# Expert stage of a decoder step: small and large items for singles and pairs, wider weight rows, every sixth weight subtraction on POOL

## The chip, the cores and the metric

The kernel runs on one core of a Trainium2 chip. The metric is the device time of one execution in microseconds (us). The engines are named as in the profile: PE (TensorE, matmuls), PEld (its weight loads), DVE (VectorE), ACT (ScalarE), POOL (GpSimd), SP (SyncE, which issues the weight loads). SBUF is the memory on the core with 128 partitions, PSUM holds the results of matmuls in eight banks of 512 columns.

## The reference

One inference step of a two-layer decoder on 256 prompt tokens and 8 sample tokens, in fp32. Layer 0 is attention and a dense SwiGLU, layer 1 a convolution module and a mixture of experts, and each sub-layer is modulated and normalised. The change is in the mixture of experts alone:

```python
logits = (h @ w_router + b_router).astype(jnp.float32)
top_l, top_e = lax.top_k(logits, MOE_TOPK)          # 2 of 8 experts for each token
gates = jax.nn.softmax(top_l, axis=-1)
...
def expert_group(args):
    xg, e = args
    return (jax.nn.silu(xg @ w1[e]) * (xg @ w3[e])) @ w2[e]
```

w1 and w3 of an expert are 1024 x 3584, w2 is 3584 x 1024, 44.04 MB together. The 264 tokens make 528 assignments. The reference's own router, evaluated on its inputs, gives the experts 0 to 7 these numbers of tokens: 5, 67, 165, 3, 200, 18, 15, 55.

## The kernel before

**Precision.** fp32 weights and activations are split into a high half (rounded to fp32r) and a low half (what remains), and a product is made of three fp32r matmuls: high by high, high by low, low by high. So each weight tile passes three engines: SP loads it into one of seven slots of `ring` (128 x 2048, 1 MB), ACT casts it to `w_hi` (L1061), DVE subtracts `w_hi` from it to `w_lo` (L1683), PE multiplies by both. The slot is free for SP when `w_lo` is written; a buffer of `w_hi` and `w_lo` is free for ACT when PE has used it.

**Units.** An expert has `ES` = 42 slots, and a slot is two units of 1024 columns, so 84 units. `SPLITS` = 4 buffers hold units. The slots of w1 and w3 hold four rows of 512 columns (2 KB pieces of a weight row), those of w2 two rows of 1024 columns (4 KB). `EXPERT_SLOTS` is the order: w1 and w3 of hidden chunk j (512 of 3584 columns, seven chunks), then w2 of chunk j - 1.

**Items.** DVE computes the list of items at run time. Of each expert up to 128 tokens are a single item; an expert of 1 to 7 with more than 128 tokens is a pair item, two groups of 128 that share each load. Expert 0 begins before the list is known. All engines run the same program of passes, `passes`: `item` for each single, `between`, then `pair` for each pair.

**A single pass** on PE: for each unit 6 matmuls with 128 tokens stationary and 512 weight columns moving (L777 for w1 and w3, L768 for w2). Behind a chunk's w3, ACT takes silu of h1 (L1071), DVE multiplies by h3 (L1718), PE transposes the product (L792, `TURN` units later), ACT and DVE split it (L1075, L1722). At the end of a pass come the gather of the next item's tokens (L741: 24 fp32 matmuls, tokens by a one-hot selection matrix), its split (L1039, L1664), and the y matmuls (L803: eight, results by the gates back to token order), each added to `zT` by DVE (L1676) before the second next may run.

**A pair pass**: w1 and w3 tiles are stationary and 2 x 128 tokens move (L852, 24 matmuls of 256 columns in a unit), w2 moves (L839, 12 matmuls of 512 columns in a unit). Subtractions are L1755, casts L1090, the gather is L813 (48 fp32r matmuls of 256 columns) and y is L873 and L874.

**Order.** Every engine runs its own instructions strictly in the order in which they are written. POOL makes constants and stores and has nothing to do in the expert stage. SP issues load n when slot n - 7 is free.

Of the kernel before, what the change touches and what calls it, by code (L numbers as in the profile page):

```python
# [16 lines left out]
F32 = mybir.dt.float32  # L17
# [22 lines left out]
EJ = FE // 512  # L40
GROUPS = 3
ITEMS = GROUPS * NE
CANDS = ITEMS + NE
PAIRS = min(2 * T // (P + 1), NE - 1)
MIN_SINGLES = NE - PAIRS
MAX_ITEMS = NE + 1 + 2 * T // (2 * P + 1)
LIST = MAX_ITEMS + PAIRS + 1
# [20 lines left out]
EXPERT_SLOTS = []  # L68
for _j in range(EJ + 1):
    _kinds = (["w1", "w3"] if _j < EJ else []) + (["w2"] if _j else [])  # L70
    EXPERT_SLOTS += [(_k, _j - (_k == "w2"), _h) for _k in _kinds for _h in range(2)]
ES = len(EXPERT_SLOTS)
EU = ES * UNITS


def last_unit(kind, j):

    return UNITS * (EXPERT_SLOTS.index((kind, j, 1)) + 1) - 1


def build(nc, x_prompt, x_sample, cache_k, cache_v, state_conv, page_table, c_prompt, c_sample,
# [5 lines left out]
    with ctx:  # L87
# [17 lines left out]
        w_hi = sb("w_hi", [P, SPLITS, UW], F32R)  # L105
        w_lo = sb("w_lo", [P, SPLITS, UW], F32R)
# [10 lines left out]
        column_v = sb("column_v", [P, CANDS])  # L117
        expert_v = sb("expert_v", [P, CANDS])
# [16 lines left out]
        arena_w = 14900  # L135
# [81 lines left out]
        x_hi2 = sb("x_hi2", [P, KC, 2, P], F32R, at=moe)  # L217
        x_lo2 = sb("x_lo2", [P, KC, 2, P], F32R, at=moe)
        g_hi2 = sb("g_hi2", [P, 2, 4, 2 * P], F32R, at=moe)
        g_lo2 = sb("g_lo2", [P, 2, 4, 2 * P], F32R, at=moe)  # L220
        x_hi, x_lo = x_hi2[:, :, 0, :], x_lo2[:, :, 0, :]
        g_hi = g_hi2[:, :, :, :].rearrange("p i c n -> p i (c n)")[:, :, 0:512]
        g_lo = g_lo2[:, :, :, :].rearrange("p i c n -> p i (c n)")[:, :, 0:512]
        g2 = sb("g2", [P, 2 * 512], at=moe)
        g_tok = g2[:, 0:512]
        h_tok = sb("h_tok", [P, 3, D], at=moe)
# [1769 lines left out]
```

## Time and profile before

| | us |
|---|---|
| median of 3 runs | 2150.91 (2150.74 to 2153.38) |
| the profiled execution, span | 2147.9 |
| PE busy | 2005.3 |
| DVE busy | 1435.4 |
| ACT busy | 1039.7 |
| POOL busy | 17.0 |
| first and last matmul of the expert units | 771.2 and 2113.9 |

The span is from the first to the last instruction. Matmuls are pipelined, so that their busy times overlap and the time between the starts of two is what one costs. In the windows view a line has the stretch, its length, busy time and count of each engine, the granted clock of TensorE (1.00 is 2.4 GHz, 0.50 is 1.2 GHz), the share of time in which the DMA engines were busy, and GB/s. In groups of instructions a line has line, engine, operation, output and inputs by name and shape, count, busy us and mean ns, and the idle time before them with what ended it.

### The profile page before, as it was taken

How to read it: one execution, taken by the hardware profiler on the slowest of the kernel's cores; microseconds unless marked ns; L12 is line 12 of the kernel's file. 1: busy time of each engine (PE TensorE's matmuls, PEld its weight loads, DVE VectorE, ACT ScalarE, POOL GpSimd, SP SyncE). 2: the span in 40 equal slices, each digit the busy share in tenths (PEclk: the TensorE clock that was granted, in tenths of full speed). 3: DMA queues.
4: the chain of work that ended last, by engine and by line, in shares of the span. 5: the costliest groups of instructions: out<-in, count | busy, mean ns of one | idle time of the engine just before them, and what ended most of it. 6: DMA issues, size and time to landing. Idle time of an engine off the chain costs nothing.

```text
span 2147.9 us, 31958 instructions
## 1 busy us (share of the span) xinstructions
PE 2005.3 (93%) x12022; PEld 1697.5 (79%) x12022; DVE 1435.4 (67%) x1928; ACT 1039.7 (48%) x1253; POOL 17.0 (1%) x68
## 2 busy tenths in 40 slices
PE   4988689999798799999999999999989999999997
PEld 2964279999787677788787887878869999799995
DVE  2578455555797579799797897978845555455454
ACT  1212223443354258677676775767724444244442
POOL 1000000000000000000000000000000000000000
PEclk8986799999898779999999999999979999999999
DMA  9647686556635059899798897998935555355520
GB/s 304 210 152 261 242 260 203 177 177 203 189 104 181 33 201 359 302 331 357 278 355 322 316 359 280 354 332 304 358 121 195 185 189 195 109 187 181 193 79 21
DMA packets 270395, 491.71 MB, mean 229 GB/s; under 512 B 9134, under 2 KB 121206, under 8 KB 270269
## 3 DMA queue, kind: packets, MB, share of 16 engines
q1 hardware_dynamic: 269261, 485.89, 65.5%
q0 software_dynamic: 1024, 4.25, 0.6%
q8 instruction: 81, 1.33, 0.3%
q14 instruction: 29, 0.24, 0.0%
HBM read 486.71 MB, written 4.35 MB: 229 GB/s over the span
## 4 chain that ended last, share of the span: by engine, by line
PE 81%; DVE 4%; ACT 1%; DMA 1%; issue 1%; DVEq 0%; SPq 0%; POOL 0%; ACTq 0%
PE banks L777 22%; PE banks L852 15%; PE banks L768 11%; PE banks L442 10%; PE banks L839 7%; PE banks L741 3%; PE banks L652 3%; PE banks L673 2%; PE banks L813 2%; PE banks L514 1%; PE banks L792 1%; PE banks L803 1%; PE banks L491 1%; PE banks L471 1%; DMA arena<-in_state_conv_dram 1%
## 5 line engine op out<-in xcount | busy, mean ns | idle before, releaser
L1683 DVE TENSOR_TENSOR w_lo<-ring,w_hi 128x1024 fp32r<-128x1024 f32 x504 | 601.1, 1222 | 72.2 <-ACT w_hi L1061 71.8
L1061 ACT CAST w_hi<-ring 128x1024 fp32r<-128x1024 f32 x504 | 521.3, 1052 | 147.5 <-PE banks L777 116.8
L1755 DVE TENSOR_TENSOR w_lo<-ring,w_hi 128x1024 fp32r<-128x1024 f32 x168 | 205.0, 1224 | 209.9 <-ACT w_hi L1090 209.0
L1090 ACT CAST w_hi<-ring 128x1024 fp32r<-128x1024 f32 x168 | 175.3, 1048 | 232.5 <-PE banks L852 169.5
L777 PE MATMUL banks<-w_hi,x_hi 128*128 128x512 f32 x672 | 268.6, 400 | 4.4 <-DVE w_lo L1683 3.2
L777 PE MATMUL banks<-w_lo,x_hi 128*128 128x512 f32 x672 | 266.5, 397 | 0.0
L777 PE MATMUL banks<-w_hi,x_lo 128*128 128x512 f32 x672 | 266.4, 396 | 0.0
L442 PE MATMUL banks<-h_hi,w_hi 128*128 128x264 f32 x800 | 237.8, 297 | 29.1 <-DVEq L404 29.1
L852 PE MATMUL banks<-x_hi,w_hi 128*128 128x256 f32 x896 | 252.3, 282 | 6.6 <-DVE w_lo L1755 6.6
L852 PE MATMUL banks<-x_hi,w_lo 128*128 128x256 f32 x896 | 251.7, 281 | 0.0
L852 PE MATMUL banks<-x_lo,w_hi 128*128 128x256 f32 x896 | 251.5, 281 | 0.0
L442 PE MATMUL banks<-h_lo,w_hi 128*128 128x264 f32 x800 | 233.5, 292 | 0.0
L442 PE MATMUL banks<-h_hi,w_lo 128*128 128x264 f32 x800 | 233.2, 291 | 0.0
L916 ACT CAST w_hi<-ring 128x1024 fp32r<-128x1024 f32 x124 | 121.5, 1031 | 199.4 <-PE banks L442 93.3
L1168 DVE TENSOR_TENSOR w_lo<-ring,w_hi 128x1024 fp32r<-128x1024 f32 x124 | 143.8, 1204 | 106.6 <-ACT w_hi L916 106.0
L442 PEld LDWEIGHTS banks<-h_hi,w_hi 128*128 128x128 f32 x800 | 158.2, 198 | 31.1 <-DVEq L404 30.7
L852 PEld LDWEIGHTS banks<-x_hi,w_hi 128*128 128x128 f32 x896 | 170.0, 190 | 7.8 <-DVE w_lo L1755 7.3
L852 PEld LDWEIGHTS banks<-x_lo,w_hi 128*128 128x128 f32 x896 | 170.0, 190 | 0.5
L852 PEld LDWEIGHTS banks<-x_hi,w_lo 128*128 128x128 f32 x896 | 169.9, 190 | 0.0
L442 PEld LDWEIGHTS banks<-h_lo,w_hi 128*128 128x128 f32 x800 | 158.3, 198 | 0.4
L442 PEld LDWEIGHTS banks<-h_hi,w_lo 128*128 128x128 f32 x800 | 157.0, 196 | 0.0
L777 PEld LDWEIGHTS banks<-w_hi,x_hi 128*128 128x128 f32 x672 | 126.8, 189 | 37.2 <-issue 6.4
(339 smaller groups left out, 3093.9 us busy)
## 6 DMA issues: line engine op xcount, KB each, us to landing
ring<-in_moe_w_dram SPq DMA_DIRECT2D x336, 1024.0 KB, 6.2
ring<-in_ada_w_dram SPq DMA_DIRECT2D x48, 1024.0 KB, 5.8
ring<-in_ffn_w_dram SPq DMA_DIRECT2D x30, 1024.0 KB, 5.5
ring<-in_attn_w_qkv_dram SPq DMA_DIRECT2D x12, 1024.0 KB, 11.9
ring<-in_conv_w_pw_dram SPq DMA_DIRECT2D x12, 1024.0 KB, 9.7
ring<-in_cache_k_dram SPq DMA_DIRECT2D x16, 512.0 KB, 6.1
ring<-in_cache_v_dram SPq DMA_DIRECT2D x16, 512.0 KB, 7.1
ring<-in_attn_w_o_dram SPq DMA_DIRECT2D x4, 1024.0 KB, 9.1
```

The source lines that it names most:

```text
L442: mm = pe.matmul(bk[:, 0:T], w, x[:, k, :], start=(k == 0 and i == 0), stop=(k == KC - 1 and i == 2))
L652: mm = pe.matmul(two[m][:, 0:T], w, x[:, g, :], start=(g == 0 and i == 0), stop=(g == FM - 1 and i == 2))
L768: mm = pe.matmul(out_b[:, b], x[:, j % 2, a], y[:, b], start=(j == 0 and u == 0 and k == 0), stop=(j == EJ - 1 and u == 3 and k == 2))
L777: mm = pe.matmul(bk[:, :], x[:, 2 * u + kk, :], y[:, b], start=(u == 0 and kk == 0 and k == 0), stop=(u == 3 and kk == 1 and k == 2))
L839: mm = pe.matmul(out_p_b[g][:, b], x[:, j % 2, u, a], y[:, b], start=(j == 0 and u == 0 and k == 0), stop=(j == EJ - 1 and u == 3 and k == 2))
L852: mm = pe.matmul(bk, x[:, a], y[:, 2 * u + kk, :, :].rearrange("p g n -> p (g n)"), start=(u == 0 and kk == 0 and k == 0 and m % 2 == 0), ...
L916: act.copy(w_hi[:, (q * UNITS + u) % SPLITS, 0:e - o], ring[:, n % RING, o:e]).then_inc(ev("w_hi_ready"), 1)
L1061: act.copy(w_hi[:, n % SPLITS, :], ring[:, pos_of(s), o:o + UW]).then_inc(ev("moe_hi_ready"), 1)
L1090: act.copy(w_hi[:, n % SPLITS, :], ring[:, pos_of(s), o:o + UW]).then_inc(ev("moe_hi_ready"), 1)
L1168: dve.tensor_tensor(w_lo[:, i, 0:e - o], ring[:, n % RING, o:e], w_hi[:, i, 0:e - o].bitcast(F32), ALU.subtract).then_inc(ev("w_lo_ready"), 1)
L1683: dve.tensor_tensor(w_lo[:, n % SPLITS, :], ring[:, pos_of(s), o:o + UW], w_hi[:, n % SPLITS, :].bitcast(F32), ALU.subtract).then_inc(ev(" ...
L1755: dve.tensor_tensor(w_lo[:, n % SPLITS, :], ring[:, pos_of(s), o:o + UW], w_hi[:, n % SPLITS, :].bitcast(F32), ALU.subtract).then_inc(ev(" ...
```

## The change

- A **small item** has up to 64 tokens. Their high and low halves stand side by side as one stationary operand of 128 columns (`x_s`), so that a product takes two matmuls in place of three: (high, low) by `w_hi` and (high, low) by `w_lo`. The halves are added when the result is turned, by a matmul with a constant `joint` of 128 x 64.
- A **large item** has up to 128 tokens and three matmuls. There are no pairs: an expert's c tokens make c // 128 large items and for the rest a small one if it is at most 64, else a large one. All small ones run first.
- A unit is now a whole slot of 2048 columns. There are `WBUF` = 3 buffers for these. Chunks are 1024 hidden columns wide (the last 512), so that w1 and w3 slots hold two rows of 1024 (4 KB pieces). 
- **POOL subtracts** for slots 3, 9, 15, 21, 27, 33 and 39 (`POOL_UNITS`), DVE for the other 35. `wait_low` waits for the one or the other.
- The gather runs on fp32r halves of the tokens behind slot 38, four before the pass's end; y matmuls of an item run in two parts inside the next item's pass, behind slots 2 and 5, and DVE adds two banks at a time.
- The first three slots are cast and subtracted before the list is computed; tokens are split at once as they leave PSUM.

The diff's core:

```diff
+CHUNKS = ((0, 2), (2, 2), (4, 2), (6, 1))
+NCH = len(CHUNKS)
+WBUF = 3
...
+TURN_AT = [n + 2 for n in LAST_W3]
+Y_AT = (2, 5)
+POOL_UNITS = tuple(range(3, ES, 6))
+
+
+def lowered(n):
+
+    mine = [i for i in range(ES) if (i in POOL_UNITS) == (n % ES in POOL_UNITS)]
+    return n % ES in POOL_UNITS, len(mine), len(mine) * (n // ES) + mine.index(n % ES) + 1
+GATE_AT, GATE_ROWS_AT, NEXT_AT, GATHER_AT = 10, 24, 24, ES - 4
...
+        def wait_low(eng, w, n):
+            on_pool, each, count = lowered(n)
+            eng.wait_ge(ev("moe_pool_lo_ready" if on_pool else "moe_lo_ready"), each * w + count)
...
+            def gather(width, x_sel, done):
+
+                x = x_b[:, 0:2 * KC * width].rearrange("p (k s n) -> p k s n", k=KC, s=2)
                 for k in range(KC):
-                    for i, (t0, tn) in enumerate(TILES):
-                        mm = pe.matmul(xT_b[:, k * P:(k + 1) * P], h_tok[0:tn, i, k * P:(k + 1) * P], sel_t[0:tn, i, :],
-                                       start=(i == 0), stop=(i == 2))
+                    for s, h in enumerate((h_tok_hi, h_tok_lo)):
+                        for i, (t0, tn) in enumerate(TILES):
+                            mm = pe.matmul(x[:, k, s, :], h[i][0:tn, k * P:(k + 1) * P], x_sel[0:tn, i, :],
+                                           start=(i == 0), stop=(i == 2), skip_group_check=True)
...
+            def x_small(k, hi, lo):
+                x = x_s[:, k, :, :].rearrange("p s n -> p (s n)")
+                return (x, hi), (x, lo)
...
+            def x_large(k, hi, lo):
+                return (x_m[:, 0, k, :], hi), (x_m[:, 0, k, :], lo), (x_m[:, 1, k, :], hi)
...
+            def small(w, first=False):
+                for n in range(ES):
+                    if n == 0:
+                        pe.wait_ge(ev("small_x_ready"), 2 * w + 2)
+                    if n in (8, 20, 32):
+                        pe.wait_ge(ev("moe_h1_kept"), NCH * w + 1 + (8, 20, 32).index(n))
+                    if n in (12, 24, 34):
+                        pe.wait_ge(ev("moe_h3_kept"), NCH * w + 1 + (12, 24, 34).index(n))
+                    unit(w, n, x_small, g_small)
+                    if n in Y_AT and not first:
+                        y_part(w - 1, Y_AT.index(n))
...
+                    if n == GATHER_AT:
+                        pe.wait_ge(ev("moe_h3_kept"), NCH * w + NCH)
+                        gather_small(w + 1)
...
+            def cast(w, n):
+                act.wait_ge(slot_sem[pos_of(n)], w * (16 * ES // RING) + moe_loaded(n))
+                act.wait_ge(ev("moe_units_used"), ES * w + n + 1)
+                act.copy(w_unit(n)[0], ring[:, pos_of(n), :]).then_inc(ev("moe_hi_ready"), 1)
...
+                    if n not in POOL_UNITS:
+                        lower(w, n)
...
             def expert(e, w, s):
 
-                sp.wait_ge(ev("moe_lo_ready"), EU * w + UNITS * (s - RING + 1))
+                wait_low(sp, w, s - RING)
                 expert_load(e, s)
...
+            def lower(w, n):
+                pool.wait_ge(ev("moe_hi_ready"), ES * w + n + 1)
+                hi, lo = w_unit(n)
+                pool.tensor_tensor(lo, ring[:, pos_of(n), :], hi.bitcast(F32), ALU.subtract).then_inc(ev("moe_pool_lo_ready"), 1)
```

How the instructions move, at three places. DVE in the first units of a single pass, before (`x_lo` is the tokens' low half, the `zT` rows are the y additions of the item before):

```order
592 L1683 TENSOR_TENSOR w_lo<-ring,w_hi 128x1024
593 L1682 REGISTER_ALU
594 L1683 TENSOR_TENSOR w_lo<-ring,w_hi 128x1024
595 L1663 ISA
596 L1664 TENSOR_TENSOR x_lo<-banks,x_hi 128x4x128 x2
597 L1673 ISA
598 L1676 TENSOR_TENSOR zT<-zT,banks 128x264
599 L1673 REGISTER_ALU
600 L1676 TENSOR_TENSOR zT<-zT,banks 128x264
```

And after, the first subtractions of a small item's pass:

```order
579 L1591 TENSOR_TENSOR w_lo<-ring,w_hi 128x2048
580 L1589 REGISTER_ALU
581 L1591 TENSOR_TENSOR w_lo<-ring,w_hi 128x2048
582 L1589 REGISTER_ALU
583 L1591 TENSOR_TENSOR w_lo<-ring,w_hi 128x2048
584 L1739 ISA
585 L1742 TENSOR_TENSOR zT<-zT,banks 128x528 x2
```

Before, the y additions (eight of 264 columns) follow the fourth unit's subtraction; after, four of 528 stand in two places further in. The three subtractions shown last are slots 2, 4 and 5: slot 3 is missing, it is POOL's.

POOL in a small item's pass, after, where it had nothing before:

```order
52 L2005 ISA
53 L2007 TENSOR_TENSOR w_lo<-ring,w_hi 128x2048
54 L2005 REGISTER_ALU
55 L2007 TENSOR_TENSOR w_lo<-ring,w_hi 128x2048
56 L2005 REGISTER_ALU
57 L2007 TENSOR_TENSOR w_lo<-ring,w_hi 128x2048
```

These are the first three of the seven subtractions of a pass, one for each sixth slot.

PE at the end of a single pass, before (`hT` is the selection matrix or the kept output, L741 the gather, L803 the y matmuls):

```order
4284 L768 MATMUL banks<-w_hi,g_lo 128x512
4285 L741 MATMUL banks<-hT,h_tok 128x128 x24
4286 L803 MATMUL banks<-hT 128x264 x2
4287 L801 REGISTER_ALU
4288 L803 MATMUL banks<-hT 128x264
```

And after, at slot 38 of a small pass (the first of eight equal groups of the gather, L768) and at the pass's end:

```order
3931 L834 MATMUL banks<-w_lo,g_buf 128x512
...
3933 L768 MATMUL banks<-sel_s,h_hi 128x64 x2
3934 L768 MATMUL banks<-sel_s,h_tok_hi 128x64
3935 L768 MATMUL banks<-sel_s,h_lo 128x64 x2
3936 L768 MATMUL banks<-sel_s,h_tok_lo 128x64
...
3991 L834 MATMUL banks<-w_lo,g_buf 128x512
3992 L374 UNCONDITIONAL_BRANCH
```

The gather has moved ahead of the last three slots, and nothing but the branch stands between the last expert matmul of a pass and the next pass.

## Rows read from the trace of the kernel before

**Rows 1.** The page: its span, and the chain that ended last.

```profile
span 2147.9 us, 31958 instructions
...
PE 81%; DVE 4%; ACT 1%; DMA 1%; issue 1%; DVEq 0%; SPq 0%; POOL 0%; ACTq 0%
PE banks L777 22%; PE banks L852 15%; PE banks L768 11%; PE banks L442 10%; PE banks L839 7%; PE banks L741 3%; PE banks L652 3%; PE banks L673 2%; PE banks L813 2%; PE banks L514 1%; PE banks L792 1%; PE banks L803 1%; PE banks L491 1%; PE banks L471 1%; DMA arena<-in_state_conv_dram 1%
```

**Rows 2.** Windows: a stretch of a single pass, and one of a pair pass.

```profile
1062.00:1160.00 98.00, 98.00 (x435) 79.08 (x434) 88.92 (x86) 75.86 (x81) 0.00 (x0) 1.00 0.99 357
1610.00:1835.00 225.00, 225.00 (x1632) 211.57 (x1631) 118.27 (x111) 96.40 (x93) 0.00 (x0) 1.00 0.57 189
```

**Rows 3.** Timeline of PE (start, length) at pass ends, and L777's first start.

```profile
1030.87 8.40 PE L741 MATMUL banks<-hT,h_tok 128*128 128x128 f32 x48
1039.20 1.16 PE L803 MATMUL banks<-hT 128*128 128x264 f32 x4
1041.01 3.62 PE L803 MATMUL banks<-hT 128*128 128x264 f32 x12 [0.65 <-DVE zT L1676]
...
1166.11 8.40 PE L741 MATMUL banks<-hT,h_tok 128*128 128x128 f32 x48
...
L777 PE MATMUL banks<-w_hi,x_hi x672: 392/396/766, 771.2 to 1559.1; 128*128 128x512 f32 x168
```

**Rows 4.** Timeline of PE: two matmuls six apart, one unit.

```profile
1102.79 0.40 PE L768 MATMUL banks<-w_hi,g_hi 128*128 128x512 f32 x1
...
1104.19 0.40 PE L768 MATMUL banks<-w_hi,g_hi 128*128 128x512 f32 x1
```

**Rows 5.** Groups on DVE and ACT in the pass from 1030 to 1166 us.

```profile
L1683 DVE TENSOR_TENSOR w_lo<-ring,w_hi 128x1024 fp32r<-128x1024 f32 x86 | 102.8, 1223 | 12.9 <-ACT w_hi L1061 12.9
L1722 DVE TENSOR_TENSOR g_lo<-banks,g_hi 128x512 fp32r<-128x512 f32 x7 | 4.8, 691 | 0.5
...
L1061 ACT CAST w_hi<-ring 128x1024 fp32r<-128x1024 f32 x85 | 88.0, 1052 | 26.1 <-PE banks L777 20.4 <-PE banks L768 5.7
...
L1075 ACT CAST g_hi<-banks 128x512 fp32r<-128x512 f32 x7 | 4.1, 588 | 5.5 <-PE banks L792 5.5
```

**Rows 6.** Waits of SP's queue from 1060 to 1160 us: total, times, longest.

```profile
SPq L1864 <- DVE w_lo L1683: 77.4, 34, 3.3
```

**Rows 7.** DMA from 225 to 245 us in 40 slices, GB/s: cache loads.

```profile
GB/s 0 0 0 0 0 0 0 164 287 270 385 401 393 393 360 401 393 410 303 352 410 418 401 401 442 434 418 401 401 451 434 410 401 369 148 66 0 0 0 0
```

**Rows 8.** Groups on POOL.

```profile
L1961 POOL MEMSET zT<- 128x2112 f32 x1 | 1.9, 1858 | 69.8 <-DVEq L404 69.8
...
L1921 POOL TENSOR_SCALAR_AFFINE_SELECT arena<-arena 128x256 f32<-128x256 f32 x1 | 0.4, 400 | 0.1
...
L1921 POOL TENSOR_SCALAR_AFFINE_SELECT arena<-arena 128x128 f32<-128x128 f32 x1 | 0.3, 294 | 0.1
```

**Rows 9.** L1595 on DVE: duration ns, start.

```profile
L1595 DVE TENSOR_SCALAR xT<-xT x1: 1246/1246/1246, 746.5 to 746.5; 128x2112 f32<-128x2112 f32 x1
```

**Rows 10.** Timeline: first weight load and last matmul of a pair's gather.

```profile
1834.84 0.19 PEld L813 LDWEIGHTS banks<-sel_p,h_hi 128*128 128x128 f32 x1
...
1843.56 0.28 PE L813 MATMUL banks<-sel_p,h_tok_lo 8*128 8x256 f32 x1
```

**Rows 11.** Timeline of PE: last gather of the singles, first pair matmul.

```profile
1571.43 8.40 PE L741 MATMUL banks<-hT,h_tok 128*128 128x128 f32 x48
...
1608.16 0.58 PE L852 MATMUL banks<-x_hi,w_hi 128*128 128x256 f32 x1 [3.98 <-DVE w_lo L1755]
```

**Rows 12.** The chain behind the last expert matmul (start, length).

```profile
2113.88 1.24 DVE out_p L1775
...
2122.11 0.46 PE banks L874 x2
```

**Rows 13.** Windows: a stretch without matmuls, and the next but one.

```profile
540.00:543.00 3.00, 0.00 (x0) 0.00 (x0) 2.96 (x6) 0.34 (x1) 0.00 (x0) 1.00 1.10 349
...
546.00:549.00 3.00, 2.93 (x13) 2.94 (x14) 2.46 (x4) 0.00 (x0) 0.00 (x0) 0.50 1.10 347
```

More of the change, by code:

```diff
@@ L877, in _, with gather_small, gather_large, y_part @@
-            passes(pe, expert, pair, lambda last: gather_pair(0))
+                        mm.then_inc(done, 1)
+            def gather_small(w):
+                pe.wait_ge(ev("small_sel_ready"), w + 1)
+                gather(SMALL, sel_s, ev("small_x_filled"))
+            def gather_large(d):
+                pe.wait_ge(ev("large_sel_ready"), d + 1)
+                gather(P, sel_m, ev("large_x_filled"))
+            def y_part(w, part):
+                if part == 0:
+                    pe.wait_ge(ev("moe_out_kept"), w + 1)
+                    pe.wait_ge(ev("moe_gs_kept"), w + 1)
+                    pe.wait_ge(ev("moe_y_zeroed"), 1)
+                else:
+                    pe.wait_ge(ev("moe_y_added"), 4 * w + 2)
+                for k in range(4 * part, 4 * part + 4):
+                    mm = pe.matmul(y_bank(k), out_sb[:, k * P:(k + 1) * P], gs[:, :], start=True, stop=True)
+                mm.then_inc(ev("moe_y_filled"), 1)
@@ L878, in _, with between @@
+            gather_small(0)
+            def between(n_small):
+                pe.wait_ge(ev("small_x_ready"), 2 * n_small + 4)
+                gather_large(0)
+            last = items(pe, lambda: small(0, first=True), lambda d: small(d + 1), between,
+                         lambda d, n_small: large(d, n_small + d + 1))
+            y_part(last, 0)
+            y_part(last, 1)
             norm(4, zT, hT, range(KC))
@@ L1110, in _, with between @@
+            for n in range(WBUF):
+                cast(0, n)
+            keep_small(0)
+            def between(n_small):
+                keep_large(0)
+            last = items(act, lambda: small(0, first=True), lambda d: small(d + 1), between,
+                         lambda d, n_small: large(d, n_small + d + 1))
+            keep_out(last)
             norm(4, zT[:, :, :], hT[:, :, :])
@@ new lines, in _ @@
+            dve.wait_ge(small_step, 1)
+            for i in range(3):
+                last = dve.tensor_scalar(sel_s[:, i, :], iota_slot[:, 0:SMALL], rank_c[:, i:i + 1], None, ALU.is_equal)
+            last.then_inc(ev("small_sel_ready"), 1)
+            for n in range(WBUF):
+                lower(0, n)
+            step(dve.memset(scan[:, :, :], 0.0))
+            step(dve.tensor_scalar(xT[:, :, :], xT[:, :, :], ALPHA, None, ALU.mult))
+            step(dve.tensor_scalar(cnt[:, 0:1], cnt[:, 0:1], float(-SMALL), None, ALU.add))
@@ L1789, in _, with between @@
+            def between(n_small):
+                dve.wait_ge(ev("moe_gsel_ready"), n_small + 1)
+                select_large(0, n_small + 1)
+            last = items(dve, lambda: small(0, first=True), lambda d: small(d + 1), between,
+                         lambda d, n_small: large(d, n_small + d + 1))
+            add_y(last, 0)
+            add_y(last, 1)
             dve.drain()
```

802 lines of the change are left out of this document (377 added, 425 removed).

## The prediction

> **What bounds the kernel now.** I read the page first: PE is busy for 93% of a span of 2147.9 us and makes 81% of the chain that ended last, with the expert stage's matmul lines L777 and L852 at its head [rows 1]. Everything the change touches is that stage, so I next read it in stretches. In a single pass (one item alone) PE is busy throughout at full granted clock while DMA moves 357 GB/s; in a pair pass PE is again full and DMA moves 189 GB/s [rows 2]. The starts of two gathers, one pass apart, give the period of a single pass: 1166.11 - 1030.87 = 135.2 us [rows 3]. Six matmuls of 512 columns take 1.40 us, 0.233 us each [rows 4], so the 84 units of a pass take 117.6 us; the other 17.6 us are a gather (8.4), the y matmuls (1039.2 to 1044.6, 5.4) and transposes (3.8) [rows 3]. PE sets both kinds of pass. DMA is not late: in a stretch of 100 us SP waits 77 for DVE to free a slot [rows 6].
>
> The stage begins with PE's first unit at 771.2 and ends with the last matmul at 2113.88: 1342.7 us for six single passes and two pair passes [rows 3, 12]. The counts follow from 504 and 168 subtractions at 84 a pass.
>
> **The new list of passes.** The router's counts, 5, 67, 165, 3, 200, 18, 15 and 55, give small items for experts 0, 3, 5, 6, 7 and the rest of expert 2: six. Large ones are experts 1, 2 and twice 4: four. Ten passes instead of eight, so 440 MB of expert weights instead of 352, and 420 instead of 336 slots to split.
>
> **A large pass.** The arithmetic per slot is two old units: 12 matmuls, 2.80 us [rows 4]. 42 slots: 117.6 us. Transposes stay 3.8. The y matmuls of the pass before need no wait between them any more, and eight at 0.29 (four took 1.16 before the first wait [rows 3]) are 2.3 us. The gather becomes 48 fp32r matmuls of 128 columns; 48 of 256 columns took 8.9 us [rows 10], half the columns would be 4.5 at least, and I take 6.4. Sum 130.1 us. DVE and ACT have the time: one subtraction of 2048 columns, from 690 ns at 512 and 1223 at 1024, is 2.29 us, and one cast, from 588 and 1052, 1.98 us [rows 5].
>
> What is new is **the slot that POOL subtracts**. With three buffers instead of four half-sized ones, the cast of slot n starts when PE has used slot n-3. PE then has 5.6 us of other work. Cast 1.98, POOL's subtraction, and about 0.4 for three hand-overs must fit into it, so POOL may take 3.2 us. No row shows POOL subtracting. Its one-tensor rows run at 0.84 ns a column (affine select 400 - 294 over 128 columns; a memset of 2112 in 1.86 us) plus 0.19 [rows 8]: 1.9 us if both reads and the write overlapped, 3.6 if the two reads follow one another, 5.4 if all three do. I take the middle of the last two, 4.5 us. Then PE stalls 4.5 - 3.2 = 1.3 us seven times a pass, 9.1 us. At the first turn (behind slot 9, which is POOL's) the product on DVE comes behind subtraction 10 and is about 0.8 us late, other turns 0.2 twice. A large pass: 130.1 + 9.1 + 1.2 = 140.4, four 562 us.
>
> The Trainium skill prices this one operation: "GPSIMD Engine Reference", section on elementwise cycle accounting, measured a two-input fp32 operation of 2048 columns at 4497 ns on GpSimd and 2293 on DVE. By it the sum is the one above; no row here shows it.
>
> **A small pass.** Its eight matmuls a slot are 1.87 us of PE, 78.4 us a pass; with 56 small turn matmuls, gather and y about 95. ACT: 42 casts of 1.98 are 83, with copies about 97. DMA: a burst of 1 MB loads ran at 390 to 410 GB/s [rows 7], so 44.04 MB need 110 us. If DVE and POOL subtract independently, DVE has 35 x 2.29 = 80 and 10.6 of its own, and DMA is last. If they can't overlap, the two together have 35 x 2.29 + 7 x 4.5 = 111.7, 14 hand-overs of 0.13 (1.8), the part of DVE's own work that no POOL slot covers (7.4 of 10.6: the y additions behind slot 8, two products and the gate copy lie beside POOL), and about 4 where ACT's copies delay a cast by more than the 0.5 us slack of three buffers. Sum 125 us, last.
>
> Which one? No row shows both reading SBUF in earnest at once. But DVE's one-input L1595 does 2112 columns in 1.25 us, 0.59 ns a column [rows 9], where a two-input subtraction needs 1.04 [rows 5]. This looks like an engine with two read paths, both taken by the subtraction of two SBUF tensors, and POOL must get its operands somewhere. I take no overlap, and keep 110 as the other end. Six small passes: 6 x 125 = 750. The first has three subtractions done ahead, and DVE computes the list among the others, which I set equal.
>
> The Trainium skill speaks against this edit more plainly. "SBUF — State Buffer", section "Who interferes with whom", says that a DVE instruction with two SBUF inputs and a GpSimd instruction that reads SBUF share a read interface, and the one issued second waits until the first is done. By that rule six passes are the 750 above, without it some 660. No row of this trace can show it.
>
> **Start, bridge, end.** The new first gather has 48 short fp32r matmuls instead of 24 fp32 ones, and three slots are cast and subtracted before it is done: I take -4, within 5 either way, so the first unit is at 767. Between the last single and the first pair PE has 36.8 us from the last gather to the first pair unit [rows 11]. Between small and large there is one gather (6.4), two copies of x (1.1 behind the last half), one cast (1.98) and one subtraction (2.29), and as PE idles for some 5 us the clock may fall: 15 us. Behind the last expert matmul (2113.88) 34.0 us are left; the 16 y matmuls from 2115.1 to 2122.6 [rows 12] become 8, their 7.4 us become 2.3: 29.
>
> **The sum.** 767 + 750 + 15 + 562 + 29 = 2123 us of span, against 2147.9. The median of the runs is 3.0 above the profiled span: 2126 us, -1.2%. The gain is small because the two pair passes (1608.2 to 2113.9, 506 us) turn into four large ones (562), and because a small pass wins only 10 us on 135, where its matmuls alone would win 39.
>
> **Rivals.** *Overlap*: POOL and DVE don't hinder one another; DMA bounds small passes at 110 and one or two for the boundary. Six, with seven slots loaded ahead (-18), 648 to 655 instead of 750. Time 2126 - 100 = 2026. For it: no row shows an obstacle. Against: the widths argument above. Chance 0.22.
>
> *Faster POOL without overlap*: at 3.6 us a slot, 0.9 x 42 = 38 in small passes and 0.9 x 28 = 25 in large: 2063. Chance 0.08.
>
> *Slower, POOL's price*: the same mechanism pays 7 us for each 0.1 us that POOL takes longer (70 slots, all on a path that ends last). The gain of 25 is used up at 4.85 us; at the bound of 5.4 the time is 2126 + 63 = 2189. For it: three streams that don't overlap at all is what the rates of one-stream rows can't exclude. Chance 0.15.
>
> *Slower, the clock*: small passes leave PE idle a third of the time. In the trace the clock stayed at its higher level in a stretch without any matmul and was at the lower, 1.2 GHz, soon after [rows 13]. At 1.2 GHz a slot needs 3.73 us and the pass some 187 instead of 125; more than two fifths of one pass at that level in total eats the gain. Against it: PE's longest gap in my small pass is 4.5 - 1.87 = 2.6 us, behind which a dense burst follows, and at 1.2 GHz PE would be busy all the time. Chance 0.05; at a fifth of the small time, 2126 + 75 = 2201.
>
> **Chances and range.** My forecast's own case has 0.50, within 2106 to 2148, and I give it 0.42 faster, 0.06 same, 0.02 slower. (About 0.2%, 4.3 us, is what a measurement of this kernel can tell from no change.) With the rivals: faster 0.42 + 0.22 + 0.08 = 0.72, same 0.07, slower 0.21. The range 2020 to 2175 takes in the overlap case and the lower half of the expensive POOL; the clock and POOL's upper bound lie outside.
>
> **What would show each step.** POOL's row should read about 4.5 us for 128x2048, and DVE's subtractions 2.29. If there is no overlap, DVE's instruction next to a POOL one either reads longer than 2.29 or waits, and a small pass's DMA moves about 350 GB/s, not 400. A large pass should take 140 us with seven idle gaps of PE released by POOL's w_lo, and a small pass 125, released by DVE or POOL, not DMA. I am wrong in the number of passes if there are not 420 loads; wrong in the rest if large passes don't show the stall, or if the page shows PE's clock below 0.9 in small passes.

## The result, and the profile after

The changed kernel takes 2235.02 us (median of 4 runs, 2226.63 to 2239.54) against 2150.82 (median of 4) for the kernel before, a ratio of 1.0385 with a 95% interval of 1.0356 to 1.0414. I had forecast 2126 us and a range up to 2175. It is slower by 84 us, where I had it faster by 25.

The page of the profiled execution: span, busy time, the chain that ended last, and the costliest groups (columns as in [rows 5]).

```profile
span 2237.8 us, 27910 instructions
...
PE 1977.1 (88%) x10382; PEld 1605.1 (72%) x10382; DVE 1538.6 (69%) x1534; ACT 1153.0 (52%) x1020; POOL 340.2 (15%) x141
...
issue 47%; PE 24%; POOL 12%; DVE 3%; ACT 2%; DMA 0%; POOLq 0%; DVEq 0%; SPq 0%; ACTq 0%
...
L1591 DVE TENSOR_TENSOR w_lo<-ring,w_hi 128x2048 fp32r<-128x2048 f32 x350 | 911.1, 2631 | 333.2 <-ACT w_hi L1074 333.2
L1074 ACT CAST w_hi<-ring 128x2048 fp32r<-128x2048 f32 x420 | 796.5, 1909 | 406.1 <-PE banks L846 295.4
L2007 POOL TENSOR_TENSOR w_lo<-ring,w_hi 128x2048 fp32r<-128x2048 f32 x70 | 322.4, 4606 | 1118.5 <-ACT w_hi L1074 1118.5
L846 PE MATMUL banks<-w_hi,x_s 128*128 128x512 f32 x672 | 298.9, 445 | 104.9 <-POOL w_lo L2007 85.0
```

In [rows 1] PE made 81% of the chain. This chain follows POOL's own queue: POOL has 12% of it, and most of the 47% called issue is the time between two of POOL's subtractions, to which the profile puts no cause, so the shares don't say what bounds the stage. The last group does say something: the small items' matmuls wait 85 us for POOL's low halves. The count is as forecast: 350 + 70 = 420 subtractions, ten passes.

ACT copies a pass's finished output (L1101) once in the next pass, so the starts of these copies give the periods. Timeline rows (start, length) of a small and a large pass:

```profile
911.30 1.01 ACT L1101 COPY hT<-banks 128x1024 f32<-128x1024 f32 x1
1045.89 1.00 ACT L1101 COPY hT<-banks 128x1024 f32<-128x1024 f32 x1
...
1768.44 1.01 ACT L1101 COPY hT<-banks 128x1024 f32<-128x1024 f32 x1
1914.94 1.01 ACT L1101 COPY hT<-banks 128x1024 f32<-128x1024 f32 x1
```

134.6 us for this small pass (the four between the first and the fifth copy are 134.6, 139.4, 136.0, 140.6, mean 137.7), 146.5 for this large one. These two periods are the measure in the experiments: small is the mean of those four, large the mean of the second and third of the four large passes.

**One POOL slot in a small pass** (timeline of POOL, DVE, PE and ACT; in brackets the idle time before and who ended it):

```profile
986.23 4.62 POOL L2007 TENSOR_TENSOR w_lo<-ring,w_hi 128x2048 fp32r<-128x2048 f32 x1 [12.21 <-ACT w_hi L1074]
...
986.34 0.43 DVE L1747 COPY hT<-banks 128x264 f32<-128x264 f32 x1
988.39 6.81 DVE L1591 TENSOR_TENSOR w_lo<-ring,w_hi 128x2048 fp32r<-128x2048 f32 x2 [1.62 <-ACT w_hi L1074]
...
990.90 0.50 PE L846 MATMUL banks<-w_hi,x_s 128*128 128x512 f32 x1 [2.31 <-POOL w_lo L2007]
...
993.74 1.90 ACT L1074 CAST w_hi<-ring 128x2048 fp32r<-128x2048 f32 x1 [3.21 <-PE banks L846]
```

POOL works from 986.2 to 990.85. DVE's copy out of PSUM (L1747) runs beside it in its usual 0.43 us. The next two subtractions take 6.81 us together instead of 4.57, and the first of them is the long one: it ends 2.15 us after POOL, nearly its usual length, so it stood still until POOL was done. PE is idle for 2.31 us and ACT, which waits for a free buffer, for 3.21.

**The gather in a small pass** (timeline of PE, then windows, in which the third number from the end is the granted clock, then DVE):

```profile
1025.25 0.30 PE L768 MATMUL banks<-sel_s,h_hi 128*128 128x64 f32 x2
...
1036.95 0.80 PE L834 MATMUL banks<-w_hi,g_buf 128*128 128x512 f32 x1
```

```profile
1025.20:1028.20 3.00, 3.00 (x18) 2.54 (x17) 3.00 (x1) 0.00 (x0) 1.06 (x1) 1.00 1.02 410
1029.70:1037.20 7.50, 7.50 (x26) 6.47 (x26) 2.29 (x1) 1.90 (x3) 0.00 (x0) 0.50 0.97 338
```

```profile
1031.01 2.29 DVE L1591 TENSOR_TENSOR w_lo<-ring,w_hi 128x2048 fp32r<-128x2048 f32 x1 [1.37 <-ACT w_hi L1074]
1042.38 2.29 DVE L1591 TENSOR_TENSOR w_lo<-ring,w_hi 128x2048 fp32r<-128x2048 f32 x1 [9.08 <-ACT w_hi L1074]
```

The 48 short matmuls take 11.70 us here, 10.9 to 12.6 in the other small passes. PE is busy all the time, yet the granted clock falls from 1.00 to 0.50 (2.4 to 1.2 GHz) in the middle of them. While they run PE frees no buffer. ACT casts one more slot at 1029.08, and the next only at 1040.44, when the first slot behind the gather, at half clock, has freed its buffer; DVE is idle for 9.08 us. ACT's own order stops it too: the cast of the gathered tokens stands ahead of the next weight cast and waits until 1037.06 for the gather.

### The profile page after: what moved, and what is told of

It reads as the page before. It is cut to its first block, busy times and chain, and to the rows that moved or that the text cites. A ratio compares the mean times of both kernels' runs of the same rounds, so it can differ in the third digit from the quotient of the medians.

```text
span 2237.8 us, 27910 instructions
## 1 busy us (share of the span) xinstructions
PE 1977.1 (88%) x10382; PEld 1605.1 (72%) x10382; DVE 1538.6 (69%) x1534; ACT 1153.0 (52%) x1020; POOL 340.2 (15%) x141
## 3 DMA queue, kind: packets, MB, share of 16 engines
q0 software_dynamic: 1024, 4.25, 0.6%
## 4 chain that ended last, share of the span: by engine, by line
issue 47%; PE 24%; POOL 12%; DVE 3%; ACT 2%; DMA 0%; POOLq 0%; DVEq 0%; SPq 0%; ACTq 0%
POOL w_lo L2007 12%; PE banks L471 11%; PE banks L681 3%; PE banks L702 2%; PE banks L846 2%; PE banks L834 1%; PE banks L768 1%; PE banks L543 1%; ACT w_hi L1074 1%; PE banks L520 1%; PE banks L500 1%; DVE w_lo L1214 1%; PE banks L804 0%; DMA ring<-in_attn_w_o_dram 0%; DVE rstd L1298 0%
## 5 line engine op out<-in xcount | busy, mean ns | idle before, releaser
L1591 DVE TENSOR_TENSOR w_lo<-ring,w_hi 128x2048 fp32r<-128x2048 f32 x350 | 911.1, 2631 | 333.2 <-ACT w_hi L1074 333.2
L1074 ACT CAST w_hi<-ring 128x2048 fp32r<-128x2048 f32 x420 | 796.5, 1909 | 406.1 <-PE banks L846 295.4
L2007 POOL TENSOR_TENSOR w_lo<-ring,w_hi 128x2048 fp32r<-128x2048 f32 x70 | 322.4, 4606 | 1118.5 <-ACT w_hi L1074 1118.5
L846 PE MATMUL banks<-w_hi,x_s 128*128 128x512 f32 x672 | 298.9, 445 | 104.9 <-POOL w_lo L2007 85.0
L846 PE MATMUL banks<-w_hi,x_m 128*128 128x512 f32 x896 | 290.5, 397 | 28.2 <-POOL w_lo L2007 22.4
L834 PE MATMUL banks<-w_hi,g_buf 128*128 128x512 f32 x784 | 297.1, 420 | 3.1 <-DVE w_lo L1591 2.5
L846 PE MATMUL banks<-w_lo,x_s 128*128 128x512 f32 x672 | 284.8, 424 | 0.0
L834 PE MATMUL banks<-w_lo,g_buf 128*128 128x512 f32 x560 | 231.2, 413 | 0.0
L964 ACT CAST w_hi<-ring 128x1024 fp32r<-128x1024 f32 x124 | 121.4, 1031 | 198.6 <-PE banks L471 92.6
L1214 DVE TENSOR_TENSOR w_lo<-ring,w_hi 128x1024 fp32r<-128x1024 f32 x124 | 143.9, 1205 | 105.7 <-ACT w_hi L964 104.8
```

Source lines behind the costliest of these rows:

```text
L834: mm = pe.matmul(out_b[:, b, :], g, y, start=(p == 0 and t == 0 and i == 0), stop=(p == NCH - 1 and t == 2 * last + 1 and i == len(g_passe ...
L846: mm = pe.matmul(bk[:, b, :], x, y, start=(k == 0 and i == 0), stop=(k == KC - 1 and i == len(x_passes(k, hi, lo)) - 1), skip_group_check= ...
L964: act.copy(w_hi[:, (q * UNITS + u) % SPLITS, 0:e - o], ring[:, n % RING, o:e]).then_inc(ev("w_hi_ready"), 1)
L1074: act.copy(w_unit(n)[0], ring[:, pos_of(n), :]).then_inc(ev("moe_hi_ready"), 1)
L1214: dve.tensor_tensor(w_lo[:, i, 0:e - o], ring[:, n % RING, o:e], w_hi[:, i, 0:e - o].bitcast(F32), ALU.subtract).then_inc(ev("w_lo_ready"), 1)
L1591: dve.tensor_tensor(lo, ring[:, pos_of(n), :], hi.bitcast(F32), ALU.subtract).then_inc(ev("moe_lo_ready"), 1)
```

## The experiments

Two questions were open: what does POOL's slot cost and by which mechanism, and what does the gather cost. All ratios are against the kernel before.

| | small | large | time | ratio (95%) |
|---|---|---|---|---|
| the changed kernel | 137.7 | 146.5 | 2235.0 | 1.0385 (1.0356 to 1.0414) |
| no subtraction on POOL | 122.7 | 138.4 | 2109.7 | 0.9808 (0.9769 to 0.9848) |
| gather in four groups | 133.7 | 141.0 | 2186.7 | 1.0174 (1.0146 to 1.0203) |
| both of these | 120.0 | 133.6 | 2083.8 | 0.9696 (0.9668 to 0.9724) |
| DVE copies, POOL subtracts | 136.4 | 143.4 | 2217.4 | 1.0320 (1.0284 to 1.0355) |
| a third of the gather | 129.1 | 132.9 | 2106.3 | 0.9788 (0.9772 to 0.9805) |
| POOL subtracts half a slot | 121.1 | 138.3 | 2102.0 | 0.9781 (0.9765 to 0.9797) |
| POOL works for nobody | 140.0 | 150.7 | 2249.4 | 1.0463 (1.0445 to 1.0481) |
| both edits, DVE copies | 111.0 | 131.8 | 2012.1 | 0.9358 (0.9304 to 0.9411) |
| both edits, three matmuls in small | 140.2 | 133.6 | 2200.0 | 1.0248 (1.0221 to 1.0274) |
| no POOL, a third of the gather | 111.6 | 126.4 | 1981.5 | 0.9222 (0.9206 to 0.9239) |

### No subtraction on POOL

```diff
-POOL_UNITS = tuple(range(3, ES, 6))
+POOL_UNITS = ()
```

> All 42 subtractions of a pass run on DVE, nothing else changed. Theory (DVE's two-input subtraction and POOL's do not overlap, and PE stalls at POOL's slots): a large pass loses its seven stalls of about 1.3 us, 146.4 to about 137 us; a small pass loses 7 x (4.60 - 2.29 + 0.26) = 18 us, 137.5 to about 120. Time 2235 - 6 x 18 - 4 x 9 = about 2090 us. Rival (POOL relieves DVE, and the small pass is long for another reason, the gather in it): DVE gets 7 x 2.29 = 16 us more work in a small pass, which stays at 135 or more; time 2200 or more.

Measured: 2109.7 us, small 122.7, large 138.4. The theory had 2090, 120 and 137, its rival 2200 or more. Moving a sixth of the subtractions to POOL costs 15.0 us in a small pass (2.1 for each of seven slots), 8.1 in a large one, and 125 us in all. By itself it makes the difference between a ratio of 0.98 and one of 1.04.

### The gather in four groups

```diff
-GATE_AT, GATE_ROWS_AT, NEXT_AT, GATHER_AT = 10, 24, 24, ES - 4
+GATE_AT, GATE_ROWS_AT, NEXT_AT, GATHER_AT = 10, 24, 24, (36, 37, 38, 39)
...
-                    if n == GATHER_AT:
-                        pe.wait_ge(ev("moe_h3_kept"), NCH * w + NCH)
-                        gather_large(d + 1)
+                    if n in GATHER_AT:
+                        i = GATHER_AT.index(n)
+                        pe.wait_ge(ev("moe_h1_kept" if i < 2 else "moe_h3_kept"), NCH * w + NCH)
+                        gather_large(d + 1, range(2 * i, 2 * i + 2))
```

> The gather's 48 short matmuls are made in four groups of 12, behind slots 36, 37, 38 and 39 instead of all behind slot 38; POOL keeps its seven slots. Theory (the unbroken run of short matmuls brings the granted clock to 0.50, and holds all three buffers meanwhile): the clock stays at 1.00, 48 matmuls take 0.19 to 0.21 us each instead of 0.24 to 0.30, the casts go on between the groups: a small pass falls by 6 to 9 us from 137.5, a large one by 4 to 6 from 146.4; time about 2165 us. Rival (the clock falls wherever short matmuls stand, in groups too): each pass keeps a stretch at 0.50 of 8 us or more, and the time stays within 15 us of 2235.

Measured: 2186.7 us, small 133.7, large 141.0. That is 4.0 and 5.5 us less for each pass with the same matmuls; the theory had 6 to 9 and 4 to 6, and a total of 2165, so it was too large for small passes. The clock stays up through the gather in three of the four small periods: of the four three are 132.0 to 133.3 us and one is 137.5, and in that one the windows at its end read

```profile
1157.00:1160.00 3.00, 3.00 (x11) 2.39 (x11) 2.29 (x1) 0.53 (x2) 0.00 (x0) 0.71 0.13 52
1160.00:1163.00 3.00, 3.00 (x11) 2.55 (x11) 0.00 (x0) 0.00 (x0) 0.00 (x0) 0.50 0.76 255
```

The groups make the fall rarer; they don't rule it out, and the falls at POOL's slots stay.

### Both edits

> Both edits: no subtraction on POOL, gather in four groups. Theory (two separate costs): small pass 110 to 114 us, where the loads bound it, large pass about 132; time about 2035 us. Rival (both edits take away the same stall): the time is within 10 us of the better one of the two single edits.

Measured: 2083.8 us, small 120.0, large 133.6. The large pass is as the theory had it, the small one 6 us longer than its 110 to 114. In a small pass the edits nearly add up: POOL costs 13.7 here and 15.0 with the gather in one piece, the grouping gives 2.7 here and 4.0 with POOL. In the whole time they add up less well: 125 and 48 us each by itself, 151 together. They are two costs with some overlap, and the rival, which had them as one, falls. This version is faster than both kernels, by 3.0% against the kernel before.

Windows of a large pass, first in this version and then in the one that has no subtraction on POOL but the gather in one piece, show what the grouping gave: the granted clock is 1.00 instead of 0.95.

```profile
1646.00:1780.00 134.00, 132.86 (x602) 108.60 (x601) 107.81 (x64) 89.75 (x54) 0.00 (x0) 1.00 0.90 329
```

```profile
1663.00:1803.00 140.00, 138.86 (x605) 113.29 (x604) 108.29 (x64) 90.38 (x54) 0.00 (x0) 0.95 0.86 317
```

### DVE copies beside POOL's subtractions

```diff
-                dve.tensor_tensor(lo, ring[:, pos_of(n), :], hi.bitcast(F32), ALU.subtract).then_inc(ev("moe_lo_ready"), 1)
+                dve.tensor_copy(lo, ring[:, pos_of(n), :]).then_inc(ev("moe_lo_ready"), 1)
```

> DVE's 35 subtractions of a pass become copies of the ring to w_lo (one input, same shape, same waits; the low halves of the weights are left out), POOL still subtracts its seven. Theory (two SBUF inputs on DVE shut POOL out and the other way round): DVE's copies run beside POOL at their usual length, a small pass falls to 115 to 122 us, a large pass stays near 146 since POOL's own 4.6 us cause its stall; time about 2120 us. Rival (POOL's length alone is the cost, DVE beside it is not held): DVE's faster instruction changes nothing that is late; small pass 133 or more, time 2205 or more.

Measured: 2217.4 us and 136.4 in a small pass. The numbers are the rival's, but its words "DVE beside it is not held" are wrong. Two things follow. My picture of the lock-out was too narrow: a copy with one input is held as well. Timeline of POOL and DVE:

```profile
1059.96 4.55 POOL L2007 TENSOR_TENSOR w_lo<-ring,w_hi 128x2048 fp32r<-128x2048 f32 x1 [13.02 <-ACT w_hi L1074]
...
1061.73 3.86 DVE L1591 CAST w_lo<-ring 128x2048 fp32r<-128x2048 f32 x1 [2.98 <-ACT w_hi L1074]
```

The copy's median is 1227 ns; this one ends at 1065.59, 1.08 us behind POOL's end. The Trainium skill ("SBUF — State Buffer", section "Who interferes with whom") lists copies and casts among the DVE instructions that can take the interface shared with GpSimd; by that rule, the trace agrees, and I had drawn on its sentence on two-input instructions only.

And the sum of DVE's and POOL's work isn't what holds this pass: 35 x 1.22 + 7 x 4.57 + 10.6 is 85 us, and the pass takes 136. With three buffers, POOL's 4.57 us stand in the chain from cast to matmul in full. The held copy adds nothing to it at this slot: PE, which had waited 3.00 us for POOL, is busy with POOL's slot until 1067.58, and the copy is done at 1065.59.

### Half a slot on POOL

```diff
-                pool.tensor_tensor(lo, ring[:, pos_of(n), :], hi.bitcast(F32), ALU.subtract).then_inc(ev("moe_pool_lo_ready"), 1)
+                lo, hi, w32 = lo[:, 0:1024], hi[:, 0:1024], ring[:, pos_of(n), 0:1024]
+                pool.tensor_tensor(lo, w32, hi.bitcast(F32), ALU.subtract).then_inc(ev("moe_pool_lo_ready"), 1)
```

> The changed kernel, but POOL subtracts only the first 1024 columns of its seven slots (the other low halves are left as they were), so that its instruction takes about 2.4 us, as long as DVE's. Theory A (the price of POOL's slot is its length in the chain of three buffers): a small pass returns to 122.7 us, the value without POOL, or a few below, a large one to 139; time 2090 to 2115 us. Theory B (the lock-out between DVE and POOL is the price, whatever its length): a small pass keeps half of the 14.8 us, 130; time 2150.

Measured: 2102.0 us, small 121.1, large 138.3; POOL's instruction takes 2428 ns. This is theory A's forecast: with an instruction on POOL that is as long as DVE's, the passes are those without POOL, within 1.6 us. They are hardly better either, though 16 us of subtractions a pass are taken off DVE, and DVE is hardly held (its subtractions have a mean of 2312 ns instead of 2288). My serial sum fits as well, since 35 x 2.29 + 7 x 2.43 is 97 us and 42 x 2.29 is 96; it is the run with DVE's copies that speaks against that sum.

```profile
L2008 POOL TENSOR_TENSOR w_lo<-ring,w_hi 128x1024 fp32r<-128x1024 f32 x70 | 169.9, 2428 | 1137.1 <-ACT w_hi L1074 1137.1
```

### POOL works for nobody

```diff
+                for n in range(3, ES, 6):
+                    pool.wait_ge(ev("moe_hi_ready"), ES * w + n + 1)
+                    for q in range(4):
+                        c = slice(512 * q, 512 * q + 512)
...
+                        pool.tensor_tensor(spare[:, :], h_hi.rearrange("p c t -> p (c t)")[:, c].bitcast(F32), h_lo.rearrange("p c t -> p (c t)")[:, c].bitcast(F32), ALU.subtract).then_inc(ev("pool_idle"), 1)
```

> All subtractions on DVE as in the run without POOL, and POOL, from the second pass on, subtracts 4 x 512 columns of constant SBUF data into a spare tile when slots 3, 9, 15, 21, 27, 33 and 39 have been cast; nobody waits for it. Theory B (POOL's work and DVE's subtractions shut one another out): DVE's instructions beside it read up to 4.5 us, a small pass goes from 122.7 to 130 or more, time 2150 or more. Theory A (only the length of what PE waits for counts): small pass 123 +- 1, time 2110 +- 5.

Measured: 2249.4 us, small 140.0, large 150.7, against 2109.7, 122.7 and 138.4 without this work. Theory B's forecast, and by more than it said: 28 instructions that nobody waits for cost 17 us in a small pass and 12 in a large one. The groups of DVE and POOL, and the durations of POOL's (min/median/max):

```profile
L1592 DVE TENSOR_TENSOR w_lo<-ring,w_hi 128x2048 fp32r<-128x2048 f32 x420 | 1109.5, 2686 | 188.6 <-ACT w_hi L1075 188.2
L2016 POOL TENSOR_TENSOR spare<-h_hi,h_lo 128x512 f32<-128x512 f32 x252 | 756.5, 3002 | 703.9 <-ACT w_hi L1075 689.1
```

```profile
L2016 POOL TENSOR_TENSOR spare<-h_hi,h_lo x252: 1260/3221/4484, 891.9 to 2193.2; 128x512 f32<-128x512 f32 x126
```

DVE's subtraction has a mean of 2686 ns instead of 2288. POOL's 512 columns take 1260 ns when nothing is in their way, and up to 4484 when they wait for DVE. So both mechanisms are real: the lock-out costs a small pass 17 us with nobody waiting for POOL, and POOL's length holds it up where DVE has time to spare (the run with DVE's copies). In the changed kernel they cover the same microseconds, and which of them sets the 15 us can't be told there. Part of the 15 us is the clock as well (below).

### A third of the gather

```diff
-                        for i, (t0, tn) in enumerate(TILES):
-                            mm = pe.matmul(x[:, k, s, :], h[i][0:tn, k * P:(k + 1) * P], x_sel[0:tn, i, :],
-                                           start=(i == 0), stop=(i == 2), skip_group_check=True)
+                        for i, (t0, tn) in list(enumerate(TILES))[2:]:
+                            mm = pe.matmul(x[:, k, s, :], h[i][0:tn, k * P:(k + 1) * P], x_sel[0:tn, i, :],
+                                           start=True, stop=True, skip_group_check=True)
```

> The changed kernel with POOL as it is, but of the gather's 48 matmuls only the 16 of the third token tile are made (the other 256 tokens' values are left out). Theory (the run of short matmuls costs its own length and brings the clock to 0.50 behind itself): no stretch at 0.50 at the ends of passes; the gather goes from 11.7 to about 3.1 us in a small pass and from 13.5 to 3.3 in a large one: small pass 137.5 to about 127, large one 146.4 to about 134; time 2235 - 63 - 50 - 9 = about 2113 us. Rival (the clock falls there for another reason, such as the waits at POOL's slots): stretches at 0.50 stay at the ends of passes, large passes stay above 140, time above 2160.

Measured: 2106.3 us, small 129.1, large 132.9, near the theory's 2113, 127 and 134. The 16 that are left take 1.9 us. Thirty-two short matmuls less are worth 8.6 us in a small pass, where I had counted PE's work as hidden altogether, and 13.6 in a large one. The grouping alone, which changes no matmul, gives 5.5 us in a large pass.

### The same without POOL

The last edit and `POOL_UNITS = ()`.

> No subtraction on POOL, and of the gather's 48 matmuls only the 16 of the third token tile, behind slot 38 (the other tokens' values are left out). Theory (the long gather holds all three buffers and stops casts and subtractions, whatever engine is the bound, and adds to POOL's price): a small pass goes from 122.7 to about 114 us, a large one from 138 to about 125; time about 1995 us. Rival (a gather on PE lies beside DVE's work once POOL's stalls are gone): small pass 120 or more, time 2050 or more.

Measured: 1981.5 us, small 111.6, large 126.4. As the theory had it (1995, 114, 125). In the first of these small periods DVE is busy for 102.2 of 111.9 us and the DMA share is 1.02 at 394 GB/s, so that the loads bound it too:

```profile
874.50:986.40 111.90, 104.39 (x487) 80.26 (x485) 102.16 (x64) 90.37 (x62) 0.00 (x0) 0.98 1.02 394
```

The full gather adds 11.1 us to a pass in which PE isn't the bound, and perhaps more if the loads left room for it. What the gather does is seen in how long DVE's subtractions stood idle for a cast, for all passes, with the full gather and with a third of it (both without POOL):

```profile
L1591 DVE TENSOR_TENSOR w_lo<-ring,w_hi 128x2048 fp32r<-128x2048 f32 x420 | 946.2, 2288 | 253.6 <-ACT w_hi L1074 253.0
```

```profile
L1591 DVE TENSOR_TENSOR w_lo<-ring,w_hi 128x2048 fp32r<-128x2048 f32 x420 | 945.8, 2287 | 136.7 <-ACT w_hi L1074 136.4
```

253.0 us against 136.4.

### Both edits, and DVE copies

> The version without POOL and with the gather in four groups, with DVE's 42 subtractions turned into one-input copies (the low halves of the weights are left out), 1.22 us instead of 2.29 us each. Theory (in a small pass DVE's 2.29 us a slot, behind the cast and with three buffers, sets the 119 us, the loads come next): small pass 110 to 113 us, large pass 131 to 133; time about 2040 us. Rival (the loads bound the small pass already, since their engines are busy for 96% of it): small pass 117 or more, time 2070 or more.

Measured: 2012.1 us, small 111.0, large 131.8. With DVE's instruction at 1.22 us the loads bound a small pass, at the 110 us that I had worked out from [rows 7]:

```profile
871.00:979.00 108.00, 105.47 (x511) 85.78 (x509) 60.19 (x63) 89.04 (x60) 0.00 (x0) 0.98 1.03 404
```

So 9 of the 120.0 us of the faster version are DVE's. I take it that with a short instruction DVE catches up after the gather and with the long one (96 of 120 us) it can't; no run shows this by itself.

### Both edits, three matmuls in small items

```diff
-                return (x, hi), (x, lo)
+                return (x, hi), (x, lo), (x, hi)
...
-                return (g, hi), (g, lo)
+                return (g, hi), (g, lo), (g, hi)
```

> The version without POOL and with the gather in four groups, but a small item makes three matmuls for each weight tile, as a large one does (the high one twice, so the products are not the reference's); what is left of the small item is its turn and its shorter gather. Theory (two matmuls in place of three take PE off the path and show in full up to the next bound): small pass from 119 to about 136 us, time about 2185 us. Rival (PE is hidden behind DVE and the loads): small pass under 125, time under 2120.

Measured: 2200.0 us, small 140.2, large unchanged at 133.6. Two matmuls in place of three are worth 20.2 us a small pass, 116 us in all. With the same gather in four groups, POOL's subtractions cost 103 us (2186.7 against 2083.8), nearly as much as this gains.

## Why the prediction was wrong

The stage by its own marks, expected and measured: first unit 767 and 771.3; six small passes 750 and 828.3 (to the first large gather at 1599.6); the bridge 15 and 19.7 (to 1619.3); four large passes 562 and 586.8 (to 2206.1); the end 29 and 31.7. The five misses, 4.3 + 78.3 + 4.7 + 24.8 + 2.7, make the 114.8 us between 2123 and 2237.8.

- **Right: the list of passes**, 420 slots, and that DVE and POOL don't work side by side. That POOL takes 4.5 us a slot: 4546 to 5007 ns, median 4595. The Trainium skill's figure ("GPSIMD Engine Reference", section "Elementwise — side-by-side cycle accounting") is 4497; by that, the trace agrees within 2.2%.
- **Right in size: POOL's price.** My sum for a small pass is 111.7 + 1.8 + 7.4 with POOL and 96.2 + 10.6 without, 14.1 us; measured 15.0, with some of the clock's falls in it, for which I had nothing. For a large pass I had 9.1, measured 8.1: the stall is 1.24 us where I had 1.3, but it came at five slots instead of seven, one of them 0.66. The mechanism was half of it: I took the serial work of two engines for the bound, and the run with DVE's copies shows that POOL's length in the chain of three buffers is enough by itself. The conclusion that I should have drawn from my own sum, and didn't, is that the same pass without POOL would be 14 us shorter.
- **Wrong: the gather in a large pass, and this is the step "half the columns ... I take 6.4".** It takes 12.4 to 13.5 us; the shortest of the four:

```profile
1744.05 0.33 PE L768 MATMUL banks<-sel_m,h_hi 128*128 128x128 f32 x2
...
1744.57 0.44 PE L768 MATMUL banks<-sel_m,h_lo 128*128 128x128 f32 x2
...
1745.19 0.44 PE L768 MATMUL banks<-sel_m,h_hi 128*128 128x128 f32 x2
...
1756.42 0.80 PE L834 MATMUL banks<-w_hi,g_buf 128*128 128x512 f32 x1
```

  I scaled [rows 10] by columns. But 48 matmuls of 256 columns took 8.9 us, 0.185 each, and the weight load shown in the same rows takes 0.19: 128 columns took no less time than 256. I read this as the weight load of each one, but no run shows it, and it isn't a fixed price: the 16 that are left in the run with a third of the gather, on 8 partitions, take 0.12 each. At the full clock three take 0.62 us here (1744.57 to 1745.19), 0.207 each, 9.9 for 48; the fall of the clock adds the rest. For the period from 1768.4 to 1914.9, 146.5 us against 140.4, the terms are: gather 13.5 (+7.1); the clock still at half for 4.3 us behind it (+2.1); y matmuls 3.9 (+1.6), because in [rows 3] an fp32 matmul has two records, 48 for the 24 of the gather, so that the four y records of 1.16 us are two matmuls and not four; POOL's stalls 5.6 for 9.1 (-3.5). That is +7.3 for a miss of 6.1: the gather with its clock is more than the miss, and POOL's smaller stalls hid a part of it. Four passes make the 24.8. The gather of the bridge, 7 us longer than the same 6.4, is more than the bridge's miss.
- **Wrong: the gather in a small pass, the step "PE ... about 95" against 111.7.** The total itself was too low: the 56 turn matmuls take 12.9 us (112 records), y 3.9 and the gather 11.7, 107 with the 78.4, and PE is busy for 116 to 122 us of a period. And I compared the engines' totals and took PE's as hidden. A total says that PE has time; it doesn't say that the others go on meanwhile. The others can fill three buffers while PE is away, and the gather keeps it away for longer, 11.7 us. 8.6 of the 13 us by which a small pass was longer than my 125 go with 32 of the gather's 48 matmuls. For the other 4 the turns (3.7 us each for three of four, 1.9 for the last) and the clock behind POOL's gaps are the candidates; no run takes these away by themselves, but the next point gives the clock a price.
- **Wrong: the clock, the step "PE's longest gap in my small pass is ... 2.6 us, behind which a dense burst follows".** I gave it a chance of 0.05. The gaps came as long as that, 2.1 to 3.1 us, and the clock fell all the same behind 22 of the 31 above 1 us. Windows around the end of the POOL subtraction that began at 950.18:

```profile
952.00:955.00 3.00, 0.56 (x3) 0.21 (x2) 3.00 (x1) 1.90 (x1) 2.74 (x1) 0.93 0.93 321
955.00:958.00 3.00, 3.00 (x8) 2.35 (x9) 3.00 (x2) 0.00 (x0) 0.00 (x0) 0.51 0.84 281
958.00:961.00 3.00, 3.00 (x15) 2.46 (x14) 1.75 (x2) 2.60 (x2) 0.00 (x0) 1.00 0.99 354
```

  PE had waited for POOL for 2.44 us before 954.79, and its clock then reads 0.51 over 3 us. A longer fall comes in the gather, where PE was busy throughout. Over the six small passes, and over the four periods between their copies:

```profile
771.30:1599.60 828.30, 720.96 (x3074) 565.92 (x3075) 637.22 (x337) 536.54 (x363) 193.59 (x42) 0.89 0.86 315
...
911.30:1045.90 134.60, 116.31 (x512) 91.16 (x513) 107.03 (x57) 90.13 (x63) 32.02 (x7) 0.92 0.89 326
1045.90:1185.30 139.40, 122.16 (x518) 96.23 (x517) 107.75 (x57) 90.43 (x62) 32.22 (x7) 0.88 0.87 316
1185.30:1321.30 136.00, 118.55 (x519) 92.12 (x517) 107.58 (x57) 90.28 (x62) 32.38 (x7) 0.92 0.88 324
1321.30:1461.90 140.60, 122.43 (x514) 96.69 (x513) 107.39 (x57) 90.19 (x62) 32.14 (x7) 0.88 0.85 313
```

  0.89 is below the 0.9 that I had named as a sign of being wrong. It means some 180 of 828 us at 1.2 GHz, about a fifth, where I had said that two fifths of a single pass eat the gain; it is the very case that I priced at 2201 us. The four periods do the same work. The two at 0.88 have 12 to 14 us more at half clock than the two at 0.92 and are 4.7 us longer, 0.35 to 0.4 us for each. The version with both edits has periods of 118.3 us at 0.99 and of 124.4 at 0.93, about as much for each. By this, an estimate, the 27 us at half clock in a mean period cost some 10 of the 137.7 us. That is argued from periods side by side; no run holds the clock up with all else the same. It isn't to be added to the gather's 8.6 and POOL's 15.0, because falls are part of both: with a third of the gather the first two periods are still at 0.93 and 0.91, which by the same estimate is 6 to 9 us and enough for the 4 left open above.
- **The range.** The case that came, a longer pass with POOL at 4.5 us, was in the clock rival at 2201, and I left it outside the range with its 0.05. The other two rivals moved along POOL's time and the overlap. The gather was a choice between 4.5 and 6.4 in the text, with the row's own 8.9 left out of the bounds; with it, and with the gather as a stop of the whole chain in small passes, the range would have reached the measured time.

## What to carry to other kernels

Work on POOL beside a DVE that reads and writes SBUF is not spare capacity. Here 32 us of subtractions on POOL in a small pass took 16 off DVE and made the pass 15 longer, and 35 us (28 x 1.26) for which nobody waited made it 17 longer. With POOL's instruction as long as DVE's there was nothing to gain or lose; a shorter one wasn't tried. An engine whose total is below the bound is still not hidden when it does one long piece that holds all the buffers; such pieces are to be compared with what the buffers let the others do meanwhile. A gap in PE's work of 2 to 3 us can cost more than itself, by the clock behind it. And the time of many short matmuls is to be taken per instruction from a row, not per column.

## What the runs showed of the hardware

- DVE and POOL hold each other off for whole instructions: a subtraction of DVE reads up to 4969 ns instead of 2286, a copy up to 3903 instead of 1227, and 512 columns on POOL up to 4484 instead of 1260. DVE's instructions with one operand in PSUM aren't held: five of the 40 additions of y (L1742) began while POOL was subtracting, and they took 691 to 695 ns, as the others did. The low halves of the products (L1780) read and write SBUF alone; 12 of their 24 began beside POOL and took 4624 to 4642 ns, the others of that shape 685.

```profile
L1742 DVE TENSOR_TENSOR zT<-zT,banks x40: 689/692/705, 923.0 to 2213.3; 128x528 f32<-128x528 f32 x40
```

```profile
L1780 DVE TENSOR_TENSOR g_buf<-g_cols,g_buf x24: 426/2654/4642, 810.9 to 1583.5; 128x512 fp32r<-128x512 f32 x18, 128x256 fp32r<-128x256 f32 x6
```

- The granted clock fell from 1.00 to 0.50 behind gaps of 2 to 3 us in PE's work (2.44 us before 954.79), not behind each of them, and also while PE did matmuls of 64 or 128 columns without a pause, and rose again in the matmuls of 512 columns behind them.
- What wasn't tried: rows of 2 KB in place of 4 KB for the weights, a fourth buffer of 2048 columns, and a gather whose tokens ACT casts behind the next weight casts.
